# Attention scores of a decoder layer in 64-row matmul pairs instead of zero-padded 128-row matmuls

## What is computed

```
z = rms_norm(x) @ w_in          # 512 pool columns | q 8 heads x 64 | k 2 x 64 | v 2 x 64
pool_y = pool_scale * (multi-scale causal means of u, windows 2, 4, 8, 16, minus u) @ pool_w
q, k  = rms_norm per head
scores[q head, i, j] = q_i . k_j / 8    in blocks of 128 queries against 256 keys (own block and the one before)
probs = softmax over the band of 128 keys with a learned sink per head
x = x + concat[rms_norm(pool_y), rms_norm(probs @ v)] @ w_out
```

## Time and profile before

| | us |
|---|---|
| median of 3 runs | 938.45 (937.75 to 938.58) |
| the profiled execution, its own time | 938.35 |
| its span, first to last instruction | 936.6 |
| TensorE busy | 923.4 (99%) |
| VectorE, ScalarE, GpSimd busy | 297.9, 385.3, 414.0 |

### The profile page before, as it was taken

How to read it: one execution, slowest core, us unless ns; L and a number is a source line. 1 busy time by engine, 2 the same in 40 slices (tenths; PEclk the granted TensorE clock), 3 DMA queues, 4 the chain that set the end, 5 groups by cost and what they waited for, 6 DMA issues and landing times.

```text
span 936.6 us, 11393 instructions
## 1 busy us (share of the span) xinstructions
PE 923.4 (99%) x4104; PEld 759.6 (81%) x4104; DVE 297.9 (32%) x467; ACT 385.3 (41%) x514; POOL 414.0 (44%) x191
## 2 busy tenths in 40 slices
PE   7999999999999999999999999999999999999998
PEld 5888888888888888777788788888888888888886
DVE  6511122211100501659978532111112200410532
ACT  5734444433321421565844644433444321321641
POOL 3554444444444444345645354444444444444340
PEclk9999999999999999999999999999999999999999
DMA  8333333332332333231223143333333323332221
GB/s 251 108 113 99 102 90 94 108 90 90 107 95 90 90 112 90 60 99 34 68 68 113 54 126 103 99 90 94 107 90 91 108 93 90 99 103 90 74 73 56
DMA packets 129650, 89.25 MB, mean 95 GB/s; under 512 B 11312, under 2 KB 114776, under 8 KB 129624
## 3 DMA queue, kind: packets, MB, share of 16 engines
q1 hardware_dynamic: 129608, 88.90, 31.9%
q10 hardware_dynamic: 16, 0.00, 0.0%
HBM read 86.80 MB, written 2.10 MB: 95 GB/s over the span
## 4 chain that ended last, share of the span: by engine, by line
PE 94%; DVE 4%; issue 1%; DMA 0%; ACT 0%; DVEq 0%; ACTq 0%
PE bank L1114 31%; PE bank L1115 31%; PE bank L1116 31%; PE bank L1129 1%; DVE sumsq L745 1%; DVE h_lo L736 1%; DVE probs L923 1%; PE bank L1260 0%; DMA x_nat<-in_x 0%; PE bank L1134 0%; DVE x_t L1088 0%; DVE tmp L1087 0%; DVE pr_lo L949 0%; DVE small L931 0%; ACT h_hi L428 0%
## 5 line engine op out<-in xcount | busy, mean ns | idle before, releaser
L324 POOL TENSOR_TENSOR w_lo<-raw,w_hi 128x1024 fp32r<-128x1024 f32 x161 | 390.2, 2426 | 479.1 <-ACT w_hi L468 240.4
L1114 PE MATMUL bank<-h_hi,w_hi 128*128 128x512 f32 x848 | 335.2, 395 | 0.3 <-DVE h_lo L736 0.3
L1115 PE MATMUL bank<-h_lo,w_hi 128*128 128x512 f32 x848 | 330.7, 390 | 0.0
L1116 PE MATMUL bank<-h_hi,w_lo 128*128 128x512 f32 x848 | 330.6, 390 | 0.0
L1114 PEld LDWEIGHTS bank<-h_hi,w_hi 128*128 128x128 f32 x848 | 159.6, 188 | 36.8 <-issue 2.3
L1115 PEld LDWEIGHTS bank<-h_lo,w_hi 128*128 128x128 f32 x848 | 159.7, 188 | 34.5 <-issue 1.9
L1116 PEld LDWEIGHTS bank<-h_hi,w_lo 128*128 128x128 f32 x848 | 159.6, 188 | 33.2
L419 ACT ACTIVATE w_hi<-raw 128x1024 fp32r<-128x1024 f32 x81 | 85.7, 1060 | 223.3 <-PE bank L1116 218.6
L468 ACT ACTIVATE w_hi<-raw 128x1024 fp32r<-128x1024 f32 x80 | 84.4, 1060 | 190.9 <-PE bank L1116 190.9
L1114 PE MATMUL bank<-act_hi,w_hi 128*128 (+1 forms) x352 | 136.9, 389 | 0.0
L1115 PE MATMUL bank<-act_lo,w_hi 128*128 (+1 forms) x352 | 136.9, 389 | 0.0
(11 more groups left out here) (149 smaller groups left out, 621.5 us busy)
## 6 DMA issues: line engine op xcount, KB each, us to landing
raw<-in_ffn_w_gate SPq DMA_DIRECT2D x44, 512.0 KB, 3.7
raw<-in_ffn_w_up SPq DMA_DIRECT2D x44, 512.0 KB, 3.7
raw<-in_ffn_w_down SPq DMA_DIRECT2D x44, 512.0 KB, 3.7
raw<-in_w_ple_gate SPq DMA_DIRECT2D x8, 512.0 KB, 3.7
raw<-in_w_in SPq DMA_DIRECT2D x6, 512.0 KB, 3.7
x_nat<-in_x SPq DMA_DIRECT2D x4, 512.0 KB, 7.0
raw<-in_w_in SPq DMA_DIRECT2D x8, 256.0 KB, 3.2
raw<-in_w_out SPq DMA_DIRECT2D x4, 512.0 KB, 3.4
```

Source lines behind the costliest of these rows:

```text
L324: pool.tensor_tensor(w_lo[:, slot, :], raw[:, slot, :], f32(w_hi[:, slot, :]), ALU.subtract).then_inc(w_ready, 1)
L1114: nc.tensor.matmul(dst, a_hi, b_hi, start=first, stop=False)
L1115: nc.tensor.matmul(dst, a_hi, b_lo, start=False, stop=False)
L1116: return nc.tensor.matmul(dst, a_lo, b_hi, start=False, stop=last)
```

## The change

The padded copies go. Keys are kept once, in `k_hi` and `k_lo` [128, 512]: the four memsets go, and two 64-row roundings and two 64-row subtractions become one each of 128 rows. `scores(b, m)` now handles the two head pairs t = 2m, 2m+1 and makes, for each, three steps of two matmuls, one per group on its own 64 rows, with 256 columns (128 for b = 0), into two banks. Unit n = 2b + m uses banks 2n % 3 and (2n + 1) % 3, one per group, and waits for `s_taken` 4n - 2, which is the first half (group 0) of the row maxima of the unit before.

```diff
-            def row_max(b, t):
+            def row_max(b, m):
...
-                dve.wait_ge(s_done, QP * b + t + 1)
+                dve.wait_ge(s_done, 2 * b + m + 1)
                 for g in range(2):
-                    n = 2 * t + g
+                    for tt in range(2):
+                        n = 2 * (2 * m + tt) + g
...
-            def scores(b, t):
-                n = QP * b + t
-                pe.wait_ge(qk_ready, 3 + t)
-                if n >= 3:
-                    pe.wait_ge(s_taken, 2 * n - 4)
...
-                product(dst, q_hi[:, t, q], q_lo[:, t, q], kz_hi[:, :, key:key + width],
-                        kz_lo[:, :, key:key + width], True, True).then_inc(s_done, 1)
+            def scores(b, m):
+                n = 2 * b + m
+                pe.wait_ge(qk_ready, 2 * m + 3)
+                if n < 2:
+                    pe.wait_ge(head_ln_done, 3 + n)
+                if n == 0:
+                    pe.wait_ge(qk_scaled, 1 + QP)
+                else:
+                    pe.wait_ge(s_taken, 4 * n - 2)
+                lo, width = (P, P) if b == 0 else (0, 2 * P)
+                keys = slice(max(b - 1, 0) * P, max(b - 1, 0) * P + width)
+                q = slice(b * P, (b + 1) * P)
+                for tt in range(2):
+                    t = 2 * m + tt
+                    for q_part, k_part, first, last in ((q_hi, k_hi, True, False), (q_hi, k_lo, False, False),
+                                                        (q_lo, k_hi, False, True)):
+                        for g in range(2):
+                            rows = slice(g * HD, (g + 1) * HD)
+                            ins = nc.tensor.matmul(bank[(2 * n + g) % 3][:, tt * 2 * P + lo:(tt + 1) * 2 * P],
+                                                   q_part[rows, t, q], k_part[rows, keys], start=first, stop=last)
+                ins.then_inc(s_done, 1)
```

More of the change, by code:

```diff
@@ L384, in _ @@
             lo_of(3, C_U + 4)
+            band_mask()
+            win_sum(0)
             lo_of(0, C_POOLW + 1)
-            win_sum(0)
             win_sum(1)
@@ L538, in qk_round @@
                 act.wait_ge(qk_normed, i + 1)
[L539 to L545, removed]
+                hi = k_hi[:] if i == 0 else q_hi[:, i - 1, :]
+                nc.scalar.activation(hi, qk[i], ACT.Copy).then_inc(qk_hi_done, 1)
             def d_round(i):
@@ L616, in _ @@
             qk_square(1)
+            head_rsqrt(0)
             qk_square(2)
-            head_rsqrt(0)
+            qk_square(3)
             split(C_U + 1)
-            qk_square(3)
+            head_rsqrt(1)
             qk_round(0)
-            head_rsqrt(1)
-            head_rsqrt(2)
             qk_round(1)
             split(C_U + 2)
+            head_rsqrt(2)
+            head_rsqrt(3)
+            qk_round(2)
+            split(C_U + 3)
             qk_square(4)
-            qk_round(2)
-            head_rsqrt(3)
             qk_round(3)
@@ L631, in _ @@
             qk_round(4)
-            split(C_U + 3)
             split(C_POOLW)
+            split(C_WP)
+            softmax(0)
+            d_round(0)
             v_round()
-            softmax(0)
             softmax(1)
@@ L644, in _ @@
             d_round(2)
+            split(C_WP + 1)
             pr_round(1, 0)
@@ L1007, in _ @@
             qk_norm(4)
-            v_scale()
+            u_scale(0)
             row_max(0, 0)
             row_max(0, 1)
-            u_scale(0)
-            row_max(0, 2)
-            row_max(0, 3)
+            v_scale()
+            u_scale(1)
             max_end(0)
             row_max(1, 0)
+            d_make(0)
             row_max(1, 1)
-            row_max(1, 2)
-            row_max(1, 3)
             max_end(1)
@@ L1021, in _ @@
             v_rest()
[L1022 to L1027, removed]
             u_scale(2)
             d_make(1)
-            row_max(2, 0)
+            d_rest(0)
+            pr_rest(0, 0)
+            normalise(1)
+            pr_rest(0, 1)
+            u_scale(3)
+            d_make(2)
             d_rest(1)
             pool_rest(0)
-            u_scale(3)
-            d_make(2)
             y_gain(0)
-            row_max(2, 1)
             d_rest(2)
@@ L1041, in _ @@
             d_rest(3)
-            row_max(2, 2)
             pool_rest(1)
-            row_max(2, 3)
+            row_max(2, 0)
+            pool_rest(2)
+            row_max(2, 1)
+            max_end(2)
+            pool_rest(3)
             row_max(3, 0)
-            max_end(2)
+            y_rest(0)
             pr_rest(1, 2)
-            y_rest(0)
             pr_rest(1, 3)
-            pool_rest(2)
-            pool_rest(3)
+            normalise(2)
+            wp_add(0)
+            y_gain(1)
+            wp_add(1)
             row_max(3, 1)
-            row_max(3, 2)
-            row_max(3, 3)
-            y_gain(1)
             max_end(3)
-            wp_add(0)
-            normalise(2)
-            wp_add(1)
-            wp_add(2)
             pr_rest(2, 0)
             pr_rest(2, 1)
+            wp_add(2)
+            y_rest(1)
             wp_add(3)
-            y_rest(1)
+            pr_rest(2, 2)
             normalise(3)
+            pr_rest(2, 3)
             wp_add(4)
-            pr_rest(2, 2)
-            pr_rest(2, 3)
+            y_gain(2)
             wp_add(5)
-            y_gain(2)
             pr_rest(3, 0)
@@ L1378, in _ @@
             q3_part(0, 2)
-            head_ms(2)
-            head_ms(3)
             q3_part(2, 4)
@@ L1389, in _ @@
             u_part(0, 0, 2)
+            scores(0, 0)
+            head_ms(4)
             u_part(0, 2, 4)
```

113 lines of the change are left out of this document (44 added, 69 removed).

## The result

The changed kernel takes 945.79 us (median of 6 runs, 945.01 to 947.31) against 938.56 (6 runs, 937.75 to 938.62) on the same chips: ratio 1.0079, 95% interval 1.0068 to 1.0090. I had forecast 938.5, no change, with a range up to 941.4, and gave slower by over 1.9 us a chance of 0.27. The prediction was wrong: the kernel is slower by more than the range allows.

What follows compares the result with a forecast made beforehand. TensorE bounds the kernel, with VectorE at 94% between 420 and 458. Matmul time -4.1, waits given back on VectorE's order +4.1, rest 0: forecast 938.5 us, range 935.4 to 941.4.

Steps and rivals of the forecast that it cites:

- the bound: TensorE is busy 99% of the span; between 420 and 458 VectorE is nearly full too, 35.90 of 38.0 us.
- the first half of the replay: New orders stepped through if pairs overlap: u_scale(0) at 420.25, VectorE idling 2.0 and 1.2 us, softmax(0) near 428.2.
- the four waits that I named between 430 and 458: TensorE waits ahead of pool_map(1) (about 1.0 us), for pr_rest(1,0) (0.7), ahead of pool_map(3) (0.8), for pool_sum(3) (1.1).
- WA moves, and nothing behind it: The mixing stage ends when WA starts, at 489.25; nothing behind changes, so time moves by that start, -0.9 to +0.9.
- the one for `pool_rest(3)`: On VectorE pool_rest(3) ends at 456.8, or about 455 with half the stretching beside GpSimd gone; wp(0) starts 455.3 to 457.1.
- matmul time -4.1: On TensorE the score matmuls take 5.6 us instead of 9.7 if the two of a pair run at once.
- the two ends: Score matmuls on TensorE: pairs run at once, gain 4.1 us; or their loads follow one another, loss 0.9 or 1.5.
- the no-overlap rival: Each 64-row matmul on TensorE pays its own load: +1.0 to +2.8 us, 940.4; chance 0.30.
- the switches that I had as a rival with 0.09: Each score unit enters and leaves the 64-row form on TensorE, 16 changes of 0.16 us, 2.6; +1.6, 940.1; chance 0.09.
- VectorE's early idle: VectorE waits 2.0 us for scores(0,1) and 1.2 for u1 ahead of u_scale(1), 3.2 us idle in all.
- A: Theory of the experiments: the new orders make the loss, by the place where max_end(2) meets GpSimd's subtractions.

Runs made afterwards that it cites:

- the gated run: Changed kernel with one wait more: GpSimd starts its two 128x1024 subtractions for w_out only once max_end(2) is done; 941.71 us, ratio 1.0036.
- The filler run: Changed kernel with 16 matmuls of 512 columns, their result unused, ahead of wp(0) on TensorE; 943.96 us, ratio 1.0055.
- the two comparisons with the same orders: Padded products against pairs: 941.53 and 941.62 us in the orders of "rest first, y_sum(0) first"; 939.17 and 938.66 in those of "gated there".
- scores earlier: "rest first, y_sum(0) first" with scores(0,1) and scores(1,0) two k-steps earlier on TensorE, u_scale(1) behind row_max(1,0) on VectorE; 940.26 us, ratio 1.0018.
- gated there: "scores earlier" with one wait more: GpSimd's subtraction for w_out's fifth chunk starts only behind max_end(3); 938.66 us, ratio 1.0000.
- rest first, y_sum(0) first: Changed kernel with pool_rest(3) ahead of max_end(2) on VectorE and y_sum(0) ahead of the second and third w_out chunk on GpSimd; 941.62 us, ratio 1.0027.
- the dummy units: Changed kernel plus eight units of 12 64-row matmuls and eight 128-row matmuls ahead of wp(7): alternating (16 switches) 956.87 us, one kind after the other (2) 953.72.

## Why the prediction was wrong, point by point

**Right: the bound and the first half of the replay.** TensorE has no gap up to 420. `u_scale(0)` started at 420.53 (forecast 420.25), VectorE idled 2.15 and 1.25 us (forecast 2.0 and 1.2), `softmax(0)` started at 428.77 (428.2). Of the four waits that I named between 430 and 458 three came, 0.84 us ahead of `pool_map(1)` (the profile names no releaser), 0.33 for a `pr_rest` and 0.63 ahead of `pool_map(3)`, and two of 0.32 that I hadn't named. "WA moves, and nothing behind it" held: 6.85 against 6.8 us.

**The step that failed** is the one for `pool_rest(3)`: "then ends at 420.25 + 33.3 + 3.2 idle = 456.8 ... With half of that stretching gone it is about 455". It ended at 461.0. The idle time was right; what was wrong is the stretching. I took it as a sum over the stretch, to be carried over or halved, though the earlier trace rows show what it is: the same 128x8 instruction at 151 and at 1369 ns, so a matter of what GpSimd is doing at that very moment. The new orders put `max_end(2)` beside `pool_sum(3)` and the two chunks behind it, back to back. It took 5.5 us in place of the 1.7 of the earlier trace rows's longest plus two short ones, and `pool_rest(3)`, which I knew `wp(0)` to wait for, is directly behind it in the list. A replay instruction by instruction of VectorE against GpSimd from 450 on would have shown it: GpSimd's order and both durations (1.30 and 2.4 us) were in the trace of before, and so was the collision: the 1.37 us of the earlier trace rows end 0.02 us behind a subtraction. The Trainium skill has the rule (SBUF — State Buffer, sections SBUF: two separate sides and Who interferes with whom): VectorE and GpSimd share a pair of ports that one instruction holds exclusively from its start to its end, and the other engine is blocked meanwhile; of VectorE's instructions it holds for those with two inputs in SBUF, against a GpSimd instruction that reads SBUF, and for those that can work in a two-port mode, `tensor_scalar` among them. This trace agrees: the ends lie within 0.03 us in three cases, what reads PSUM was not stretched, and in the gated run the two instructions that met nothing took 0.17 us. I had weighed no rule for it in the prediction.

**The second part of that loss** I didn't price at all: after the wait the clock stood at its lower level for eight matmuls, 1.6 us. The filler run confirms it with 1.8.

**The mis-sized term** is "matmul time -4.1". The pairs do overlap, so I chose the right one of the two ends; the no-overlap rival is out. But the switches that I had as a rival with 0.09 are real in addition: 16 x 0.19 = 3.1 us against the 2.6 that I worked out. Net 1.0 us; the spacing in the trace gives 6 x 0.26 less 2 x 0.24 for the narrow units, 1.1. Of that TensorE's busy time shows 0.6 and 0.8 us in the two comparisons with the same orders, and about 0.6 comes back as waits in both. I had treated overlap and switching as alternatives, while they are two terms of one sum. The Trainium skill's sentence that a change of tiling mode drains TensorE (TensorEngine Tiling (Array Packing), Key Properties) stood in the prediction; the traces agree that a change costs time, 0.19 to 0.20 us each.

**The sum of the loss**, by runs: 4.1 us for the stretched `max_end(2)` with the clock behind it (gated), 1.4 for VectorE's early idle of 3.4 us (scores earlier), 1.6 for the stretched `max_end(3)` (gated there; TensorE's wait was 1.0 of it): 7.0 of 7.2 (945.79 - 941.71, 941.62 - 940.26 and 940.26 - 938.66; the first step was made in two ways, gated and by "rest first, y_sum(0) first", which differ by 0.1). The early idle I had in the forecast, and set it off in full against the gain in matmul time, which was not there. The stretched `max_end(3)` is not there in the changed kernel, where its three instructions took 0.17, 0.17 and 0.59 us; it arises once `wp(0)` is early, and is taken off the first term as it is added in the third. So the three terms hold in this order of undoing them.

**Against my forms of the theory**: A was right on the place and wrong on the remedy. The old orders do not bring the old time back with pairs (947.54), by the waits because of the banks; and each cure of the first collision brought another, on `max_end(0)` with a moved chunk, on `max_end(3)` with the other order of GpSimd and with the first gate. No run here beats the kernel before.

**Open**: why the lower clock lasted longer in some runs of the same kernel than in others; why TensorE waits some 0.6 us longer with pairs; and whether pairs with fewer switches (units put together) would pay, which the banks didn't let me try.

## What to carry to other kernels

Where two engines contend, don't carry an average of the stretching from one order to another: replay both engines over the same microseconds, and look for short instructions of the engine that sets the pace beside long ones of the other. A wait on the long one and another order each won 4.1 us here, and each brought the next collision, which took a second wait: look through the new trace for it. For a new form of matmul count the changes of form as well as the matmuls: a unit of six pairs takes 0.7 us where padded products take 1.36, and pays 0.4 of the difference for its two switches.

## What the runs showed of the hardware

- A VectorE instruction of 128x8 elements, 0.17 us alone, that starts while a GpSimd `tensor_tensor` runs ends with it: 0.96 us beside one of 128x512 that had begun 0.36 us earlier, and 2.26 to 2.32 beside 128x1024 begun 0.1 us earlier, with two SBUF inputs and also as `tensor_scalar` with one. It ended within 0.03 us of GpSimd's. Row maxima (0.42 us) and `scalar_tensor_tensor` (0.75) that read PSUM were not stretched.
- Two 64-row matmuls on different rows, each with its own weight load, cost 0.11 us (128 columns) and 0.12 us (256 columns) a pair, issued alternately or three and three (shown for 256 columns).
- A change between 64-row and 128-row matmuls costs 0.19 to 0.20 us, by the dummy units (2.70/14, and 0.40 for two).
- After 4.2 us without work on TensorE the first eight matmuls ran at the 1.2 GHz level, 0.43 us each; in the run with pairs in the old orders the level held through 462.5 to 467.5, behind a wait of 3.4 us. With 16 matmuls without use in the idle time the clock stayed at 1.00, and 1.8 us were won.
